# One transfer of 8,192 bytes per partition for each expert weight unit, and another order for the last two experts

## The reference, cut to what matters

```
def hier_moe(h, w_rg, b_rg, w_re, b_re, w_g, w_u, w_d):
    ...                      # group and expert scores, softmax, top 2 of 8 in the best of 4 groups
    def expert_block(args):
        xb, e = args
        return (jax.nn.silu(xb @ w_g[e]) * (xb @ w_u[e])) @ w_d[e]
    ...
    y = jax.ops.segment_sum(ys * row_w[:, None], row_tok, num_segments=t + 1)[:t]
```

## Time and profile before

| | us |
|---|---|
| median of 3 runs (lowest, highest) | 786.52 (786.0, 787.46) |
| the profiled execution | 787.02 |
| its span | 785.3 |
| PE busy in the span | 729.8 (93%) |
| DVE, ACT, POOL busy | 282.3, 176.1, 47.1 |
| DMA, 247.41 MB | mean 315 GB/s |
| from issue to landing of a 512 KB unit half (median) | 14.1 to 15.3 |

### The profile page before, as it was taken

How to read it: one execution, slowest core, us unless ns; L and a number is a source line. 1 busy time by engine, 2 the same in 40 slices (tenths; PEclk the granted TensorE clock), 3 DMA queues, 4 the chain that set the end, 5 groups by cost and what they waited for, 6 DMA issues and landing times.

```text
span 785.3 us, 10243 instructions
## 1 busy us (share of the span) xinstructions
PE 729.8 (93%) x3983; PEld 419.9 (53%) x3983; DVE 282.3 (36%) x460; ACT 176.1 (22%) x269; POOL 47.1 (6%) x86
## 2 busy tenths in 40 slices
PE   3999999999999895999999999999988998998896
PEld 3877799899999783533333333333323323332332
DVE  5358777744474757322121212111121112112112
ACT  4374364364444423200000000000000000000001
POOL 6002100000000002000000000000000000000000
PEclk8999999999999998999999999999999999999999
DMA  8944434443544697499999999999999999999994
GB/s 250 387 182 157 177 130 161 143 146 108 214 149 174 204 412 294 155 393 410 409 409 409 409 409 409 410 408 409 408 410 409 409 410 409 409 410 408 410 409 176
DMA packets 77648, 247.41 MB, mean 315 GB/s; under 512 B 8616, under 2 KB 8704, under 8 KB 77600
## 3 DMA queue, kind: packets, MB, share of 16 engines
q1 hardware_dynamic: 76176, 245.46, 80.8%
q0 software_dynamic: 880, 1.24, 0.9%
q10 hardware_dynamic: 544, 0.06, 0.1%
HBM read 245.67 MB, written 1.06 MB: 314 GB/s over the span
## 4 chain that ended last, share of the span: by engine, by line
PE 68%; DMA 21%; DVE 5%; SPq 2%; ACT 2%; issue 1%; DVEq 0%; ACTq 0%
PE ps L1191 19%; DMA unit<-in_w_expert_up 14%; PE ps L1217 9%; PE ps L930 6%; PE ps L931 6%; PE ps L932 6%; DMA unit<-in_w_expert_down 6%; PE ps L1228 5%; PE ps L908 3%; PE ps L910 3%; PE ps L909 3%; PE ps L1204 3%; SPq L483 2%; DMA ring<-in_w_in 2%; DVE ring_lo L1278 1%; ACT w_hi L677 1%
## 5 line engine op out<-in xcount | busy, mean ns | idle before, releaser
L1191 PE MATMUL ps<-unit,xe 128*64 128x512 f32 x512 | 234.8, 597 | 18.4 <-DMA unit<-in_w_expert_up 16.7
L1193 PE MATMUL ps<-unit,xe 128*64 128x512 f32 x512 | 235.2, 598 | 0.0
L1191 PEld LDWEIGHTS ps<-unit,xe 128*64 128x64 f32 x512 | 65.2, 136 | 176.9 <-issue 152.3
L1652 DVE TENSOR_TENSOR g_act<-g_act,ps 64x512 f32<-64x512 f32 x32 | 22.1, 692 | 288.7 <-ACT g_act L848 288.7
L1217 PE MATMUL ps<-unit,he 128*64 128x512 f32 x512 | 118.4, 595 | 3.1 <-DMA unit<-in_w_expert_down 3.0
L1278 DVE TENSOR_TENSOR ring_lo<-ring,w_hi 128x1024 fp32r<-128x1024 f32 x80 | 96.3, 1223 | 58.7 <-ACT w_hi L677 58.3
L930 PE MATMUL ps<-hT_hi,w_hi 128*128 128x256 f32 x320 | 92.6, 289 | 4.4 <-DVE ring_lo L1278 4.4
L677 ACT ACTIVATE w_hi<-ring 128x1024 fp32r<-128x1024 f32 x80 | 83.2, 1057 | 57.4 <-PE ps L932 36.2
L932 PE MATMUL ps<-hT_hi,ring_lo 128*128 128x256 f32 x320 | 91.5, 286 | 0.0
L931 PE MATMUL ps<-hT_lo,w_hi 128*128 128x256 f32 x320 | 91.3, 285 | 0.0
L1217 PEld LDWEIGHTS ps<-unit,he 128*64 128x64 f32 x512 | 35.6, 137 | 80.6 <-issue 64.5
(11 more groups left out here) (284 smaller groups left out, 745.3 us busy)
## 6 DMA issues: line engine op xcount, KB each, us to landing
unit<-in_w_expert_gate SPq DMA_DIRECT2D x128, 512.0 KB, 14.1
unit<-in_w_expert_up SPq DMA_DIRECT2D x128, 512.0 KB, 15.3
unit<-in_w_expert_down SPq DMA_DIRECT2D x128, 512.0 KB, 15.0
ring<-in_w_in SPq DMA_DIRECT2D x9, 2048.0 KB, 13.9
ring<-in_w_merge_gate SPq DMA_DIRECT2D x6, 2048.0 KB, 9.0
ring<-in_w_branch SPq DMA_DIRECT2D x3, 2048.0 KB, 8.7
ring<-in_w_out SPq DMA_DIRECT2D x2, 2048.0 KB, 8.5
x_tok<-in_x SPq DMA_DIRECT2D x2, 512.0 KB, 4.1
```

Source lines behind the costliest of these rows:

```text
L1191: t_.matmul(ps[0:WIN, b, :], xe[b][:, k, :], u[:, 0, C * j:C * (j + 1)], start=(k == 0), stop=(k == KD - 1))
L1193: ins = t_.matmul(ps[WIN:P, b, :], xe[b][:, k, :], u[:, 1, C * j:C * (j + 1)], start=(k == 0), stop=(k == KD - 1))
```

## The change

A unit is now 8,192 bytes per partition of one matrix, in one transfer: kinds `g`, `u` and `d`, two of each per expert. Down is laid out like gate and up, with four consecutive rows in a partition (`(p k)` instead of `(k p)`), so `turn_h` takes every fourth column of `g_act` (`j::KC`). A half of `gate_up` waits for a `g` and a `u` unit and frees both at its end. Expert 31 has another order: gate_up first half, turn_h(30), combine(29), down(30), gate_up second half, combine(30), turn_h(31), down(31), combine(31). The very last unit comes in two transfers with a semaphore each. The result of down(31) goes to two banks, 256 columns each, and VectorE and ScalarE copy one each. The copies to `fin` wait for their own token tile only.

```
--- before.py
+++ after.py
@@ -278,7 +278,7 @@
         unit_at = [ring_at[s] + 4 * UNIT * j for s in range(3) for j in range(2)] + spare_at
         unit_at += [ring_at[s] + 4 * UNIT * j for s in range(3, 5) for j in range(2)]
         unit_at += [w_hi_at, w_hi_at + 4 * UNIT, x_at, xn_at]
-        unit = [place(f"unit{i}", [P, 2, CW], F32, at=at) for i, at in enumerate(unit_at)]
+        unit = [place(f"unit{i}", [P, UNIT], F32, at=at) for i, at in enumerate(unit_at)]
         assert len(unit) == RING
 
         ps = ctx.enter_context(nc.psum_tensor("ps", [P, 8, 512], F32))
@@ -295,6 +295,7 @@
         small_in = sem("small_in")
         wz_in = sem("wz_in")
         landed = [sem(f"landed{s}") for s in range(PRE_RING)]
+        last_in = sem("last_in")
         unit_in = [sem(f"unit_in{i}") for i in range(RING)]
         consts = sem("consts")
         v_chain = sem("v_chain")
@@ -399,6 +400,7 @@
         hit_ready = sem("hit_ready")
         back_ready = sem("back_ready")
         combined = sem("combined")
+        y_last = sem("y_last")
         fin_act = sem("fin_act")
         fin_dve = sem("fin_dve")
         stored = sem("stored")
@@ -432,18 +434,20 @@
 
         wg_v = w_expert_gate[0].rearrange("e (p k) n -> e p (k n)", k=KD)
         wu_v = w_expert_up[0].rearrange("e (p k) n -> e p (k n)", k=KD)
-        wd_v = w_expert_down[0].rearrange("e (k p) n -> e p k n", p=P)
-
-        order = [("gu", 0, c) for c in range(4)]
+        wd_v = w_expert_down[0].rearrange("e (p k) n -> e p (k n)", k=KC)
+
+        order = [(kind, 0, c) for c in range(2) for kind in ("g", "u")]
         for e in range(1, NE):
-            order += [("gu", e, c) for c in range(4)] + [("d", e - 1, c) for c in range(2)]
+            halves = [[(kind, e, c) for kind in ("g", "u")] for c in range(2)]
+            below = [("d", e - 1, c) for c in range(2)]
+            order += halves[0] + (below + halves[1] if e == NE - 1 else halves[1] + below)
         order += [("d", NE - 1, c) for c in range(2)]
         assert len(order) == UNITS
         number = {u: n for n, u in enumerate(order)}
 
         def after(p, kind, e):
 
-            return UNITS * p + (UNITS + number[kind, e, 3 if kind == "gu" else 1] + 1)
+            return UNITS * p + (UNITS + number["u" if kind == "gu" else kind, e, 1] + 1)
 
         def uses(j):
 
@@ -475,12 +479,12 @@
 
                 kind, e, c = order[n]
                 j = n % RING
-                for i in range(2):
-                    if kind == "gu":
-                        src = (wg_v, wu_v)[i][e, :, chunk(c)]
-                    else:
-                        src = wd_v[e, :, 2 * c + i, :]
-                    sp.dma_start(unit[j][:, i, :], src).then_inc(unit_in[j], 16)
+                src = {"g": wg_v, "u": wu_v, "d": wd_v}[kind]
+                if n == UNITS - 1:
+                    sp.dma_start(unit[j][:, 0:D], src[e, :, c * UNIT:c * UNIT + D]).then_inc(last_in, 16)
+                    sp.dma_start(unit[j][:, D:UNIT], src[e, :, c * UNIT + D:(c + 1) * UNIT]).then_inc(unit_in[j], 16)
+                else:
+                    sp.dma_start(unit[j][:, :], src[e, :, c * UNIT:(c + 1) * UNIT]).then_inc(unit_in[j], 16)
 
             def first_load(n):
 
@@ -862,9 +866,12 @@
                 for e in range(NE):
                     silu(p, e)
                     he_out(p, e)
-
-            act.wait_ge(combined, passes * (4 * NE) + 8)
-            for tt in range(TT):
+                act.wait_ge(unit_free, after(p, "d", NE - 1))
+                act.wait_ge(combined, (4 * NE) * p + 4 * (NE + 1))
+                s_.activation(y_sb[:, C // 2:C], bank(2)[:, 0:C // 2], ACT.Copy).then_inc(y_last, 1)
+
+            for tt in range(TT):
+                act.wait_ge(combined, passes * (4 * NE) + (6 + 2 * tt))
                 s_.activation(fin[:, tt, 0:C], bank(4 + 2 * tt), ACT.Copy).then_inc(fin_act, 1)
 
 
@@ -1175,7 +1182,7 @@
             def landed_unit(p, n):
 
                 j = n % RING
-                pe.wait_ge(unit_in[j], 32 * uses(j) * p + (32 * (n // RING) + 32))
+                pe.wait_ge(unit_in[j], 16 * uses(j) * p + (16 * (n // RING) + 16))
                 return unit[j]
 
             def gate_up(p, e, cs):
@@ -1185,14 +1192,16 @@
                     pe.wait_ge(xe_ready, NE * p + (e + 1))
                     pe.wait_ge(h_ready, NE * p + (e + 1))
                 for c in cs:
-                    u = landed_unit(p, number["gu", e, c])
-                    for j in range(2):
-                        k = 2 * c + j
-                        t_.matmul(ps[0:WIN, b, :], xe[b][:, k, :], u[:, 0, C * j:C * (j + 1)],
-                                  start=(k == 0), stop=(k == KD - 1))
-                        ins = t_.matmul(ps[WIN:P, b, :], xe[b][:, k, :], u[:, 1, C * j:C * (j + 1)],
-                                        start=(k == 0), stop=(k == KD - 1))
-                    ins.then_inc(unit_free, 1)
+                    ug = landed_unit(p, number["g", e, c])
+                    uu = landed_unit(p, number["u", e, c])
+                    for j in range(4):
+                        k = 4 * c + j
+                        gate = t_.matmul(ps[0:WIN, b, :], xe[b][:, k, :], ug[:, C * j:C * (j + 1)],
+                                         start=(k == 0), stop=(k == KD - 1))
+                        up = t_.matmul(ps[WIN:P, b, :], xe[b][:, k, :], uu[:, C * j:C * (j + 1)],
+                                       start=(k == 0), stop=(k == KD - 1))
+                    gate.then_inc(unit_free, 1)
+                    up.then_inc(unit_free, 1)
 
             def turn_h(p, e):
 
@@ -1201,7 +1210,7 @@
                     pe.wait_ge(rows_ready, 2)
                 pe.wait_ge(he_ready, NE * p + (e + 1))
                 for j in range(KC):
-                    ins = t_.matmul(ps[:, 2, j * WIN:(j + 1) * WIN], g_act[WIN:P, j * P:(j + 1) * P],
+                    ins = t_.matmul(ps[:, 2, j * WIN:(j + 1) * WIN], g_act[WIN:P, j::KC],
                                     ident[WIN:P, WIN:P], start=True, stop=True)
                 ins.then_inc(h_turned, 1)
 
@@ -1210,18 +1219,32 @@
                 pe.wait_ge(he_ready, NE * p + (e + 2))
                 pe.wait_ge(y_ready, NE * p + (e + 1))
                 for c in range(2):
-                    u = landed_unit(p, number["d", e, c])
+                    n = number["d", e, c]
+                    if n == UNITS - 1:
+                        pe.wait_ge(last_in, 16 * p + 16)
+                    u = unit[n % RING] if n == UNITS - 1 else landed_unit(p, n)
                     for j in range(2):
                         k = 2 * c + j
+                        if n == UNITS - 1 and j == 1:
+                            u = landed_unit(p, n)
+                        if e == NE - 1:
+                            for part in range(2):
+                                for half in range(2):
+                                    at = D * j + C * half + C // 2 * part
+                                    ins = t_.matmul(ps[half * WIN:(half + 1) * WIN, 3 - part, 0:C // 2], he[:, k, :],
+                                                    u[:, at:at + C // 2], start=(k == 0), stop=(k == KC - 1))
+                            continue
                         for half in range(2):
                             ins = t_.matmul(ps[half * WIN:(half + 1) * WIN, 3, :], he[:, k, :],
-                                            u[:, j, C * half:C * (half + 1)], start=(k == 0), stop=(k == KC - 1))
+                                            u[:, D * j + C * half:D * j + C * (half + 1)], start=(k == 0), stop=(k == KC - 1))
                     ins.then_inc(unit_free, 1)
 
             def combine(p, e):
 
                 pe.wait_ge(back_ready, NE * p + (e + 2))
                 pe.wait_ge(y_ready, NE * p + (e + 2))
+                if e == NE - 1:
+                    pe.wait_ge(y_last, p + 1)
                 for tt in range(TT):
                     for half in range(2):
                         rows = slice(WIN * half, WIN * half + WIN)
@@ -1229,16 +1252,21 @@
                                   start=False, stop=True, skip_group_check=True).then_inc(combined, 1)
 
             with pe.Fori(0, passes) as p:
-                gate_up(p, 0, (0, 1, 2, 3))
-                for e in range(1, NE):
-                    gate_up(p, e, (0, 1))
+                gate_up(p, 0, (0, 1))
+                for e in range(1, NE - 1):
+                    gate_up(p, e, (0,))
                     turn_h(p, e - 1)
                     if e >= 2:
                         combine(p, e - 2)
-                    gate_up(p, e, (2, 3))
+                    gate_up(p, e, (1,))
                     down(p, e - 1)
+                gate_up(p, NE - 1, (0,))
+                turn_h(p, NE - 2)
+                combine(p, NE - 3)
+                down(p, NE - 2)
+                gate_up(p, NE - 1, (1,))
+                combine(p, NE - 2)
                 turn_h(p, NE - 1)
-                combine(p, NE - 2)
```

(7 more changed lines are left out.)

## The result

The changed kernel takes 791.55 us (median of 4 runs, 790.34 to 792.2) against 786.99 for the kernel before on the same chip (4 runs, 786.0 to 787.72). The ratio is 1.0057, 95% interval 1.0038 to 1.0076: slower by 0.57%, or 4.6 us. I had forecast 781.3 us, in a range of 777.5 to 791.0. The time lies 0.55 us above the range and on the wrong side of no change.

What follows compares the result with a forecast made beforehand. The weight stream was taken as the bound, with TensorE faster and waiting late; restart, 172 units and tail set the end. Rows -10.7, restart +1.7, tail +3.8 gave -5.2 us: 781.3 us, range 777.5 to 791 (8 in 10).

Steps and rivals of the forecast that it cites:

- The rate: Expert weight stream, 172 units: 8,192-byte rows save 62 ns per unit, 10.7 us off (0 to 13.8).
- rival C: Expert weight stream: the full packet constant, 75 ns off each unit, -12.9 us, total 779.1 us; chance 0.14.
- Rivals A and B: Expert stream: A, 4 KB packets at ceiling, 792.0 us, chance 0.12; B, 24 ns per unit, 787.9 us, chance 0.12.
- Restart: Stream's pause behind unit 19: first buffers come free after 8 passes instead of 4, +1.7 us (0 to 2.5).
- Steady experts: Expert loop on TensorE: strided turn_h costs 0.2 us more per turn, 13.45 us per expert, hidden under DMA's 15.0.
- rival D: Expert loop: strided turns, 0.93 us more each, make TensorE the bound; +2.5 us, 789.0 us; chance 0.21.
- Tail: Behind the third-last unit's landing: 20.4 us instead of 16.65, with waits before combine(30) and behind turn_h; +3.8 us (2.8 to 6).
- The sum: Whole kernel: -10.7 + 1.7 + 3.8 = -5.2 us, giving 781.3 us from a median of 786.52.

## Why the prediction was wrong

*The rate: right, a little low in size.* I took 62 ns per unit; 421 against 409 GB/s is some 71 ns (70 to 73 by the rounding), rival C's constant (75) nearly. The estimate worked out from the page "DMA: Bandwidth & Descriptors" (section "Bandwidth") of the Trainium skill was 421.5 GB/s and 72 ns, and the trace, at 421 GB/s and 71 ns, agrees. In the kernel with contiguous turns the whole 12.2 us are there: 768.65 + 1.7 - 12.2, less the 0.95 by which its stage starts earlier, is 757.2 us for the landing, and 756.84 was measured. Rivals A and B fall.

*Restart: right.* SP issues 328.29 - 324.64 = 3.65 us behind the first product (forecast 3.6; before 1.97), and the stream stands at 0 GB/s from 327 to 329 us.

*Steady experts: this is the step that failed.* "turn_h's products have 64 columns, which is nearer to L881", and so I took 0.2 us per turn. Measured are 0.98, above even my upper bound of 0.93. The load is what takes the time, 324 ns, as L1159's did, and the number of columns that pass behind it doesn't make it shorter. L881's row showed how far passes follow each other, 0.136 us each, and it is a row of transposes. The groups of loads in the trace of the kernel before, which I hadn't put side by side, tell the two kinds apart (both have a step of 32 bytes):

```profile
L1159 PEld LDWEIGHTS ps<-perm,xn_hi 128*128 128x128 f32 x16 | 5.2, 327 | 0.6 <-issue 0.4
...
L881 PEld LDWEIGHTS ps<-ident,x_tok 128*128 128x128 f32 x16 | 2.0, 193 | 0.2
```

A strided product loads in 327 ns, a strided transpose in 193, and turn_h is made of products. (Sixteen other transposes of L881, of xn_merged, load in 218 ns.) So L881 was near in its columns and far in what counts. The experiment with transposes bears this out: in turn_h they load with the same step in 209 ns in place of 324. The Trainium skill's page "SBUF — State Buffer" (section "Door 1: The DMA port swizzle") wants at least two hits in a line of 16 bytes for full bandwidth. By that a step of 8 bytes is free and one of 16 is not; the loads of 194 and 324 ns agree, while those of the transposes (193 and 209 ns with one hit in a line) don't. I had named this rule and given the row that spoke against it more weight.

The consequence was worked out rightly as rival D. With 0.98 and a first product 0.63 us earlier, its sum gives 737.9 - 0.63 + 31 x 0.98 = 767.65 us, and the trace has 767.65. That was 7.9 us behind my own arrival of 759.75, so TensorE and not the stream set the start of the tail.

*Tail: right.* 20.95 us from 767.65 to the end of the span. I had 20.3 behind the same point, and 0.7 more for a strided turn: 21.0. Step by step, with the forecast (and rival D's turn) in brackets: half of gate_up(31) 3.43 (3.6), hole 2.25 (2.2), combine 1.99 (2.0), turn 1.70 (1.93), hole behind it 0.83 (0.9), 32 passes 3.70 (3.9), halves of y with their signals 0.77 (0.65), combine 2.03 (2.0), last copy to fin 0.7 (0.7), and to the end of the span 3.5 (3.1). So the sum is right partly because small misses cancel: the steps on TensorE are shorter and the end, where I had taken 0.7 off for the first store, is 0.4 longer. The last unit's products start at 779.7 us, over 17 us after the stream's end, so the split transfer gains nothing, as forecast.

*The sum, redone from the traces.* Start of half gate_up(31) in place of a landing: 767.65 - 768.65 = -1.0. Tail: 20.95 - 16.65 = +4.3. Together +3.3, which is the difference of the spans (788.6 - 785.3). The medians are 4.6 apart: the profiled execution, 790.34 us, is the fastest of the four, and what makes the others up to 1.9 us longer no trace shows. Put as parts: the long rows alone would have brought 12.2 - 1.7, but TensorE, at 14.23 us per expert, isn't there in time to use them, and the new order's 3 to 4 us come on top. Without the stride, but with the new order, the time is 783.19 (779.7 in the runs where the clock stayed); without the new order 787.44; without both 775.29.

*The chances.* D had 0.21, and its mechanism is what happened. Its price of 789.0 us lies 1.3 under the profiled execution, and 2.6 under the median. The 1.3 are accounted for by the turns (31 x 0.05, less 0.63 for the earlier start: 0.9) and by the 0.5 that my sum took off to come from the profiled execution to the median. I gave the forecast 0.38 on the strength of one sentence about one row, and ended the range at 791, which left D's price little room for a spread of its own.

## What to carry to other kernels

When a change alters the access pattern of an operand, look for the row of the same instruction (here the load, PEld) with that pattern, and don't take the spacing of passes that may overlap it. How much room an engine has behind a stream with a head start isn't the difference of the two rates: it is the gap between its own arrival and the last landings, divided by the number of times the cost is paid (here 0.64 us, against 0.98). And where the work is reordered at an end, look at which copies lose the work that stood before their wait; here these two holes cost more than the earlier bytes could bring.

## What the runs showed of the hardware

- Loading a stationary operand of 64 partitions and 128 columns of 4 bytes took 187 ns with a step of 4 bytes, 194 with 8, 258 with 12, 324 with 16. A product's over 128 partitions with a step of 32 bytes took 327; a transpose's took 209 with 16 bytes, and 193 and 218 with 32.
- Rows of 8,192 bytes per partition moved at 421 GB/s, rows of 4,096 at 409, in the same kernel with one and two transfers per unit; one transfer of 2 MB with rows of 4,096 moved at 410.
- Writes with a step of 512 bytes slowed ScalarE's silu from 589 to 1,076 ns and VectorE's product from 691 to 1,058, each 64 x 512 elements (VectorE also read one operand with that step).
- TensorE's granted clock fell to the 1.2 GHz level (0.50) in the tail of some runs, behind an idle stretch of 3.00 us in one profile and of 2.22 in two others; in a fourth it averaged 0.57 around and behind one of 0.83. It stayed at full level behind stretches of 2.25 and 0.83 us in the changed kernel's profile, of 2.23 in the 8-byte kernel's, and of 3.00 in the one with contiguous turns and 4,096-byte rows. The length of the hole alone doesn't decide, and what does stays open. It cost 4.5 us in the first tail (2.9 of them in the 32 passes that took 6.57 in place of 3.70) and 1.6 in the fourth.
- Not tried: a second tile for the permuted product, so that only VectorE writes it with a step, and a remedy for the 1.7 us of the restart.
